# Halves and crossing products of the HGRN2 recurrence at step 14 instead of 11, its output and squares two steps later

## The reference

```python
def hgrn2_recurrence(q, k, v, logf):
    # S_t = diag(f_t) S_{t-1} + k_t v_t^T, o_t = S_t^T q_t, by chunks
    ...
        attn = jnp.einsum("bhtd,bhsd,bhtsd->bhts", q_i, k_i, decay)
        o_i = (jnp.einsum("bhtd,bhde->bhte", q_i * jnp.exp(b_i), state)
               + jnp.einsum("bhts,bhse->bhte", attn, v_i))
...
    q_raw, f_raw, i_in, z = jnp.split(x @ w_in, 4, axis=-1)
    ...
    o = hgrn2_recurrence(heads(q), heads(k), heads(i_in), heads(logf))
    o = rms_norm(o, hgrn_norm_g) * jax.nn.silu(heads(z))
    return o.reshape(bsz, s, HGRN_WIDTH) @ w_out
```

## Time and profile before

| | |
|---|---|
| Time, median of 3 runs | 901.56 us (901.53 to 902.18) |
| Profiled execution | 902.52 us |
| Its span in the profile | 900.7 us |
| PE busy | 884.0 us, 98% |
| DVE, ACT, POOL busy | 459.7, 504.7 and 668.7 us |

### The profile page before, as it was taken

How to read it: one execution, slowest core, us unless ns; L and a number is a source line. 1 busy time by engine, 2 the same in 40 slices (tenths; PEclk the granted TensorE clock), 3 DMA queues, 4 the chain that set the end, 5 groups by cost and what they waited for, 6 DMA issues and landing times.

```text
span 900.7 us, 18968 instructions
## 1 busy us (share of the span) xinstructions
PE 884.0 (98%) x7503; PEld 816.7 (91%) x7503; DVE 459.7 (51%) x979; ACT 504.7 (56%) x712; POOL 668.7 (74%) x480
## 2 busy tenths in 40 slices
PE   6999999999999999999999999999999999999997
PEld 6999999999997889999999999888997899998886
DVE  4368763485532633777768776635666442220004
ACT  5775533763336456565677656556576356664331
POOL 5986766457656888958776786769796579989882
PEclk9999999999999999999999999999999999999999
DMA  8664544435444565645444555455552357666631
GB/s 317 209 225 126 162 133 128 129 107 164 142 128 168 183 188 174 202 124 171 151 132 129 164 158 150 145 192 187 158 198 91 94 161 226 203 198 208 197 118 47
DMA packets 40824, 146.08 MB, mean 162 GB/s; under 512 B 4512, under 2 KB 4640, under 8 KB 40736
## 3 DMA queue, kind: packets, MB, share of 16 engines
q1 hardware_dynamic: 39296, 140.71, 49.5%
q10 hardware_dynamic: 1440, 4.16, 1.3%
HBM read 143.81 MB, written 1.05 MB: 161 GB/s over the span
## 4 chain that ended last, share of the span: by engine, by line
PE 90%; DVE 3%; ACT 2%; issue 2%; POOL 2%; DMA 1%; SPq 0%; DVEq 0%; ACTq 0%; POOLq 0%
PE dense L509 25%; PE dense L510 24%; PE dense L511 24%; PE bank L870 2%; POOL wlo L484 1%; PE dense L565 1%; PE bank L707 1%; POOL wlo L483 1%; PE bank L708 1%; DVE cv L1716 1%; DMA raw<-weight_units_dram 1%; PE bank L902 1%; PE bank L856 1%; ACT whi L1130 1%; PE bank L1013 1%
## 5 line engine op out<-in xcount | busy, mean ns | idle before, releaser
L484 POOL TENSOR_TENSOR wlo<-raw,whi 128x512 fp32r<-128x512 f32 (+1 forms) x259 | 409.3, 1587 | 22.7 <-ACT whi L1130 22.6
L1130 ACT ACTIVATE whi<-raw 128x1024 fp32r<-128x1024 f32 (+1 forms) x262 | 273.3, 1057 | 231.7 <-PE dense L511 198.1
L483 POOL TENSOR_TENSOR wlo<-raw,whi 128x512 fp32r<-128x512 f32 x195 | 253.7, 1301 | 179.2 <-ACT whi L1130 177.2
L509 PE MATMUL dense<-x_hi,whi 128*128 128x256 f32 x1232 | 350.3, 284 | 6.9 <-DVE wlo L1647 6.5
L510 PE MATMUL dense<-x_lo,whi 128*128 128x256 f32 x1232 | 343.0, 278 | 0.0
L511 PE MATMUL dense<-x_hi,wlo 128*128 128x256 f32 x1232 | 342.8, 278 | 0.0
L509 PEld LDWEIGHTS dense<-x_hi,whi 128*128 128x128 f32 x1232 | 232.7, 189 | 10.9 <-DVE x_lo L1636 6.5
L510 PEld LDWEIGHTS dense<-x_lo,whi 128*128 128x128 f32 x1232 | 232.9, 189 | 0.7 <-issue 0.2
L511 PEld LDWEIGHTS dense<-x_hi,wlo 128*128 128x128 f32 x1232 | 233.0, 189 | 0.0
L509 PE MATMUL dense<-whi,ya_hi 128*128 128x512 f32 x192 | 77.4, 403 | 1.0 <-issue 0.8
L511 PE MATMUL dense<-whi,ya_lo 128*128 128x512 f32 x192 | 75.0, 391 | 0.0
(11 more groups left out here) (336 smaller groups left out, 1374.5 us busy)
## 6 DMA issues: line engine op xcount, KB each, us to landing
raw<-weight_units_dram SPq DMA_DIRECT2D x261, 512.0 KB, 3.9
xtok<-in_x_dram SPq DMA_DIRECT2D x1, 1024.0 KB, 7.7
gb<-in_ln_g_dram ACTq DMA_DIRECT2D x2, 512.0 KB, 4.5
gb<-in_ln_b_dram ACTq DMA_DIRECT2D x2, 512.0 KB, 6.4
out_dram<-zt SPq DMA_DIRECT2D x3, 256.0 KB, 2.0
qT<-x_turned_dram SPq DMA_DIRECT2D x2, 256.0 KB, 4.4
raw<-weight_units_dram SPq DMA_DIRECT2D x2, 256.0 KB, 4.6
qT<-x_turned_dram SPq DMA_DIRECT2D x1, 512.0 KB, 7.1
```

The lines of the kernel that those rows point to most:

```text
L483: pool.tensor_tensor(wlo[:, slot, 0:half], unit_slot(u)[:, 0:half], whi[:, slot, 0:half].bitcast(F32), ALU.subtract)
L484: pool.tensor_tensor(wlo[:, slot, first:2 * half], unit_slot(u)[:, first:2 * half], whi[:, slot, first:2 * half].bitcast(F32), ALU.subtrac ...
L509: pe.matmul(out_, lh, rh, start=start, stop=False, skip_group_check=True)
L1130: act.activation(whi[:, u % NSPL, first:], unit_slot(u)[:, first:], ACT.Copy).then_inc(hi_done, 1)
```

## The change

For the first six pairs (`HG_LATE`), the halves and crossing products go from step 11 to step 14, which is the next pair's step 6, ahead of its diagonal and level 0; they are written to `SB[3]` instead of `SB[1]`. The output goes from step 14 to 16 and the steps behind it follow it. The last two pairs keep their steps. The waits follow: the diagonal waits for less, level 0 waits for the third level's selections of the pair before by a wait of its own, and the halves wait until the pair before has left `SB[3]` (`hg_ready`).

```diff
-HG_LAST = 11
-HG_OUT = [14] * (HH // 2 - 1) + [12]
+HG_LATE = HH // 2 - 2
+HG_LAST = [14] * HG_LATE + [11, 11]
+HG_OUT = [16] * HG_LATE + [14, 12]
...
+        def hg_halves_bank(p):
+
+            return SB[3] if p < HG_LATE else SB[1]
+
...
             def hg_diagonal(p):
 
                 pe.wait_ge(hg_q, p + 1)
-                if p > 0:
+                if p > HG_LATE:
                     pe.wait_ge(hg_picked, 5 * p)
                     pe.wait_ge(hg_cross, p)
+                elif p > 0:
+                    pe.wait_ge(hg_picked, 5 * (p - 1) + 1)
...
                 pe.wait_ge(hg_ranked, 5 * p + n + 1)
                 if n > 0:
                     pe.wait_ge(hg_picked, 5 * p + n + 1)
+                elif p > 0:
+                    pe.wait_ge(hg_picked, 5 * (p - 1) + 4)
...
             def hg_halves(p):
 
                 pe.wait_ge(hg_ranked, 5 * p + 4)
-                pe.wait_ge(hg_picked, 5 * p + 1)
+                if p >= HG_LATE:
+                    pe.wait_ge(hg_picked, 5 * p + 1)
+                elif p > 0:
+                    pe.wait_ge(hg_ready, p)
...
-                    if r == HG_LAST:
+                    if r == HG_LAST[p]:
                         hg_halves(p)
                         hg_across(p)
```

More of the change, by code:

```diff
@@ L875, in hg_halves @@
                 pe.wait_ge(hg_ranked, 5 * p + 4)
-                pe.wait_ge(hg_picked, 5 * p + 1)
+                if p >= HG_LATE:
+                    pe.wait_ge(hg_picked, 5 * p + 1)
+                elif p > 0:
+                    pe.wait_ge(hg_ready, p)
                 for u in range(4):
-                    last = pe.matmul(SB[1][0:64, u * 64:(u + 1) * 64], tokens_of(hk, p % 2, u // 2, u % 2)[:, 0:64],
+                    last = pe.matmul(hg_halves_bank(p)[0:64, u * 64:(u + 1) * 64], tokens_of(hk, p % 2, u // 2, u % 2)[:, 0:64],
                                      tokens_of(q0, p % 2, u // 2, u % 2)[:, 64:P], start=True, stop=True)
@@ L888, in hg_across @@
                         cols = slice(first + 64 * half, first + 64 * half + 64)
-                        pe.matmul(SB[1][0:64, cols], kx[:, i, :], queries, start=True, stop=True)
-                        last = pe.matmul(SB[1][64:P, cols], tokens_of(hk, p % 2, i, 0)[:, 64:P], queries, start=True, stop=True)
+                        pe.matmul(hg_halves_bank(p)[0:64, cols], kx[:, i, :], queries, start=True, stop=True)
+                        last = pe.matmul(hg_halves_bank(p)[64:P, cols], tokens_of(hk, p % 2, i, 0)[:, 64:P], queries, start=True, stop=True)
                 last.then_inc(hg_cross_mm, 1)
@@ L2120, in hg_halves @@
                 o = four(AA[0:64, p % 2, :])[:, :, 64:P]
-                link(vec.tensor_copy(o, SB[1][0:64, 0:256].rearrange("p (u c) -> p u c", u=4)), hg_picked)
-                vec.tensor_copy(CR[:, p % 2, :], SB[1][:, 2 * P:4 * P]).then_inc(hg_cross, 1)
+                link(vec.tensor_copy(o, hg_halves_bank(p)[0:64, 0:256].rearrange("p (u c) -> p u c", u=4)), hg_picked)
+                vec.tensor_copy(CR[:, p % 2, :], hg_halves_bank(p)[:, 2 * P:4 * P]).then_inc(hg_cross, 1)
                 settle(hg_cross)
```

## The result

| | before | changed |
|---|---|---|
| Median of 20 runs | 902.35 us (901.53 to 902.81) | 903.80 us (903.15 to 904.60) |
| Ratio of the runs, 95% interval | | 1.0018 (1.0012 to 1.0024) |
| Span of the profiled execution | 900.7 us | 901.5 us |

With 20 runs the median of before is 902.35 and not the 901.56 that three had given. The change costs 1.45 us; forecast were +1.3. As a time, 902.9 was forecast, and 0.8 of the 0.9 us that it is off come from that base. 903.8 lies inside the range.

What follows compares the result with a forecast made beforehand. PE was taken to bound the stage. Per pair -0.33 (merging) + 0.75 (stall) - 0.20 (spacing) = +0.22 us, six times +1.3, added to the 901.56 median: 902.9 us; range 900.2 to 905.4.

Steps and rivals of the forecast that it cites:

- PE bounds the stage, start to start is what counts: Recurrence stage: PE sets the time, changes there reach the end one for one; gaps below some 0.3 us show no idle.
- Merging the burst saves 0.33 us a pair: Step 11's burst on PE: 1.27 us goes, 0.94 is added ahead of the next pair's L856; 0.33 saved.
- Moving output and squares costs nothing: Output products and sums of squares on PE, behind later bursts: same count and kinds of transition, cost nothing.
- The chain on VectorE and the stall of 0.75: Copies delay level 0's preparation, keys and selections on DVE; PE stalls at the second burst, 0.75 us a pair.
- every landmark: DVE times from merged burst's start: copies 1.27, preparation 2.17, keys 3.54, selections end 8.46; PE's second burst 8.61 us.
- The 7.86 at which PE wants to go: Unstalled start of PE's second burst, from the merged burst's start: 6.92 plus 0.94 ahead, 7.86 us.
- The way from the last selection's end to the small matmul: From DVE's release to PE's second burst: between zero and 0.30 us, taken as 0.15.
- Spacing, -0.20 a pair: Projection matmuls in units 11 to 14: some go from 0.118 to 0.113 us; gain 0.2, ends -0.2 and +0.32.
- Rival 3, the wait for the low part: Halves in the merged burst wait for the previous pair's low part: another 0.5 us a pair, 905.9; chance 0.07.
- The other thin margin: First level frees its projection's PSUM pair near 4.4 us, for the unit starting near 5.0: margin 0.6 us, enough.

Runs made afterwards that it cites:

- e3: The changed kernel with the second copy of the crossings made twice on VectorE for the first six pairs: 907.21 us, ratio to before 1.0060.
- e5: e1 with three more copies of the crossings on VectorE for the first six pairs: 903.87 us, ratio to before 1.0021.
- e4: e1 with one more copy of the crossings on VectorE for the first six pairs: 899.02 us, ratio to before 0.9966.
- e2: The kernel before with only output, squares and what follows moved two steps later, halves still at step 11: 902.29 us, ratio 0.9999.
- e1: The changed kernel with level 0's three preparing operations ahead of the two copies on VectorE: 899.17 us, ratio to before 0.9967.

## Why the prediction was right

- **PE bounds the stage, start to start is what counts.** Held. e3 and e5 turned time added to this chain into time of the kernel, e4 showed where that begins.
- **Merging the burst saves 0.33 us a pair.** Between e2 and e1, which differ by the merging and DVE's order for it, are 3.1 us, 0.52 a pair. In e1 the merged burst puts 0.92 ahead of L863, where the own burst cost 1.27 net, so 0.33 to 0.35 are the burst and the rest is the spacing. Right in size.
- **Moving output and squares costs nothing.** Held (e2).
- **The chain on VectorE and the stall of 0.75.** Right at every landmark within 0.03 us in the pair shown. The stall is 0.76 to 0.78 in four of six pairs and 4.4 us in all, where 4.5 were forecast. The 7.86 at which PE wants to go, the sum that the stall rests on, is where it goes in e1. The way from the last selection's end to the small matmul was taken as 0.15 and is 0.14 (477.39 to 477.53). e1 and e5 confirm the cause from both sides.
- **Spacing, -0.20 a pair.** The 72 slow matmuls of a pair became 24: from 486.83 to 494.78 there are 70 steps of 0.1136 and from 495.01 to 497.60 22 of 0.118. That gives 48 at 0.0045, -0.22. Units 11 to 13 run fast, as forecast; unit 14, which ran fast before, is slow now. The prediction had no cause for the spacing and took 0.20 out of ends of -0.2 and +0.32, so that it came so near is in part luck. The Trainium skill's "TensorE: Matmul & The Clock Gate", section "Back-to-back issue gap", has one value for 256 columns, 262 cycles or an estimated 0.109 us, in its table of the isolated gap; by it this term would be nothing. The trace doesn't agree: it has two spacings, and the difference between them is this term. One pair of six met the slow spacing far longer: its merged burst starts at 527.14 and the one ahead at 497.81, 29.33 us. That is 0.42 more than the others, and explains why the stage lost 1.7 us and not six times 0.21. No term of the sum has it. The trace of e5, with the same stall, has no such pair (its matmuls at the slow spacing are about as many as in e1).
- **Rival 3, the wait for the low part.** L2166 ends at 468.30, 0.60 ahead of the merged burst at 468.90. The forecast margin was 0.7. It costs nothing here. The other thin margin, the keys' end for the second unit behind the merged burst, is 4.45 to 5.05 as forecast; e3 uses it up.

The sum for a regular pair, -0.35 + 0.77 - 0.22 = +0.20, against 28.91 - 28.70 = +0.21 measured.

What stays open is the cause of the two spacings. They switch behind some bursts and at the start of some units, in e3 at a unit that started late, but no run here isolates it.

## What to carry to other kernels

Work that is moved to save the busiest engine a pause brings its consumer along, and on the other engine's in-order list that consumer holds up everything behind it that could have run early. Before merging two bursts, write down the other engine's list from the burst's start to the release of the next one, and compare that end with the margin that the trace shows. If it comes out late, put the operations that don't need the moved work ahead of it: here that alone (e1) turned 1.5 us of loss into 3 us of gain.

## What the runs showed of the hardware

- A dependency that ends 0.28 us ahead of the next small matmul costs nothing (e4: 475.01 to 475.29); one that ends late is followed by the matmul after 0.14 us (477.39 to 477.53 in the changed kernel, 478.36 to 478.50 in e5).
- The view of waits understates a stall on PE: 4.0 us for six in the changed kernel, where start to start shows 4.4 (in the pair shown, 0.70 and 0.76).
- Identical 256-column matmuls run at 0.113 or 0.118 us from start to start at the same granted clock, in stretches of mostly 24 to 72 between two bursts. With a wait of 0.45 us more a pair, more of them were slow (e3); with e5's three copies and about the same stall as in the changed kernel, fewer.
